# A chain of mixers: part order of an output chunk, low parts in halves, roots and gates' sums moved ahead

## The reference, cut to what matters

```python
y = gla_mixer(x, ...)              # layer 0; layer 1: dsa_mixer(x, ...)
x = layer_norm(ALPHA * x + y, ln_g[i], ln_b[i])
x = x + (p[i] @ ple_w[i]) * jax.nn.sigmoid(x @ ple_gate_w[i])
...
h = rms_norm(x, norm_g) @ w_in     # the block after the layers
```

## Time and profile before

| | |
|---|---|
| median of 3 runs (lowest, highest) | 1513.79 us (1510.99, 1514.42) |
| the profiled execution: time, span | 1513.75 us, 1512.0 us |
| TensorE matmul busy | 1454.0 us, 96% |
| DVE, ACT, POOL busy | 619.2, 524.0, 553.9 us |
| mean granted clock of TensorE | 0.985 |

### The profile page before, as it was taken

One profiled execution on the slowest core, in us unless ns is written; L12 is line 12 of the kernel. 1 busy time (PEld: TensorE's weight loads), 2 busy tenths in 40 slices (PEclk: granted clock), 3 DMA queues, 4 the chain that ended last, 5 costly groups with the idle time before them and its releaser, 6 DMA issues.

```text
span 1512.0 us, 25079 instructions
## 1 busy us (share of the span) xinstructions
PE 1454.0 (96%) x10817; PEld 1269.4 (84%) x10817; DVE 619.2 (41%) x1296; ACT 524.0 (35%) x866; POOL 553.9 (37%) x235
## 2 busy tenths in 40 slices
PE   7999999999999999999999999998999999988898
PEld 7898886799998897778788899978988987768897
DVE  6032351124016335379655511454123512477424
ACT  3354223433113232333444421233434322563311
POOL 6433421133333225964373234323343342062211
PEclk9999999999999999999999999999999999998999
DMA  5222220022522123222110042223432222002111
GB/s 172 85 84 84 84 84 29 29 84 85 202 91 84 52 97 111 84 80 88 56 57 29 29 181 85 79 76 112 142 88 90 79 84 84 1 15 74 70 58 56
DMA packets 114669, 122.90 MB, mean 81 GB/s; under 512 B 12666, under 2 KB 107750, under 8 KB 114303
## 3 DMA queue, kind: packets, MB, share of 16 engines
q1 hardware_dynamic: 111008, 115.36, 23.5%
q10 hardware_dynamic: 3550, 5.94, 1.1%
HBM read 114.99 MB, written 6.31 MB: 80 GB/s over the span
## 4 chain that ended last, share of the span: by engine, by line
PE 90%; DVE 5%; ACT 2%; POOL 1%; issue 1%; ACTq 0%; DVEq 0%
PE ps L218 86%; PE ps L1454 1%; DVE x L1199 1%; DVE x L1194 1%; PE ps L1036 1%; DVE heads L2042 1%; PE ps L1460 0%; DVE qkT L2130 0%; ACTq L339 0%; ACT xT_high L909 0%; PE ps L278 0%; PE ps L900 0%; PE ps L3061 0%; POOL w_low L199 0%; PE ps L2649 0%
## 5 line engine op out<-in xcount | busy, mean ns | idle before, releaser
L199 POOL TENSOR_TENSOR w_low<-w_ring,w_high 128x2048 fp32r<-128x2048 f32 (+4 forms) x95 | 415.2, 4372 | 735.9 <-ACT w_high L184 722.8
L218 PE MATMUL ps<-w_high,xT_high 128*128 128x256 f32 (+1 forms) x1056 | 304.8, 289 | 9.0 <-POOL w_low L460 4.1
L218 PE MATMUL ps<-w_low,xT_high 128*128 128x256 f32 (+1 forms) x1056 | 299.2, 283 | 0.0
L218 PE MATMUL ps<-w_high,xT_low 128*128 128x256 f32 (+1 forms) x1056 | 299.1, 283 | 0.0
L184 ACT ACTIVATE w_high<-w_ring 128x2048 fp32r<-128x2048 f32 (+1 forms) x91 | 171.5, 1885 | 314.1 <-PE ps L218 310.0
L218 PE MATMUL ps<-xT_high,w_high 128*128 128x512 f32 (+1 forms) x600 | 241.3, 402 | 2.2 <-POOL w_low L199 1.2
L218 PE MATMUL ps<-xT_high,w_low 128*128 128x512 f32 (+1 forms) x600 | 237.0, 395 | 0.0
L218 PE MATMUL ps<-xT_low,w_high 128*128 128x512 f32 (+1 forms) x600 | 236.3, 394 | 0.0
L218 PEld LDWEIGHTS ps<-w_high,xT_high 128*128 128x128 f32 x1056 | 202.6, 192 | 16.0 <-issue 6.3
L218 PEld LDWEIGHTS ps<-w_low,xT_high 128*128 128x128 f32 x1056 | 202.7, 192 | 1.7 <-issue 1.7
L218 PEld LDWEIGHTS ps<-w_high,xT_low 128*128 128x128 f32 x1056 | 202.5, 192 | 0.0
(11 more groups left out here) (503 smaller groups left out, 2166.9 us busy)
## 6 DMA issues: line engine op xcount, KB each, us to landing
w_ring<-in_gla_w_in_dram SPq DMA_DIRECT2D x24, 1024.0 KB, 5.2
w_ring<-in_dsa_w_in_dram SPq DMA_DIRECT2D x19, 1024.0 KB, 5.0
w_ring<-in_w_in_dram SPq DMA_DIRECT2D x18, 1024.0 KB, 5.0
w_ring<-in_gla_w_out_dram SPq DMA_DIRECT2D x8, 1024.0 KB, 5.0
w_ring<-in_ple_gate_w_dram SPq DMA_DIRECT2D x8, 1024.0 KB, 4.8
w_ring<-in_dsa_w_out_dram SPq DMA_DIRECT2D x8, 1024.0 KB, 4.8
x_scratch<-x SPq DMA_DIRECT2D x4, 1024.0 KB, 6.7
w_ring<-in_w_out_dram SPq DMA_DIRECT2D x4, 768.0 KB, 4.6
```

The costliest lines, as they stand in the source:

```text
L199: ins = self.nc.gpsimd.tensor_tensor(low[:, part], whole[:, part], high[:, part].bitcast(F32), ALU.subtract)
L218: return self.nc.tensor.matmul(out, lhs, rhs, start=first, stop=last, skip_group_check=not check)
```

## The change

Six edits in one:

1. In the first output chunk, part j waits for low part 9 + j of g (of 16) instead of all four parts for 12, and `last_turns` stands behind part 1 of c = 0 instead of in front of c = 1.
2. The gate's first chunk is made low in two halves; TensorE takes the first four row tiles after the first half. POOL makes the low parts of later chunks only after all four tiles are normalised. ACT makes this chunk's high part in front of the split of the first tile.
3. On ACT the roots of tiles 0 and 1 stand behind square (1, 1), in front of the last sigmoid; the order behind the last sigmoid is final(0), root(2), final(1), square(1, 3), root(3).
4. On DVE scale(0), scale(1) and final(0) stand in front of the last gate; behind it square_sum(2), scale(2), final(1), square_sum(3), scale(3), final(2), final(3). The wait for the gain moves one tile ahead.
5. Chunk zA is made low in halves.
6. At `cum_copies` DVE does `branch_step` in front of `norm_heads`.

```diff
@@ phase_post, TensorE
-                pe.wait_ge(gT_made, gT_count + KI - 4)
                 for n in range(LAST):
...
                         if n == 0 and c == 1:
-                            last_turns(pe)
                             pe.wait_ge(*gT_done)
                         w = g.chunk(pe, first + 2 * n + c)
                         for j in range(NT):
+                            if n == 0 and c == 0:
+                                pe.wait_ge(gT_made, gT_count + KI - 8 + j + 1)
                             part(w, n, c, j).then_inc(sem["y_part"], add("y_part", 1))
+                            if n == 0 and c == 0 and j == 1:
+                                last_turns(pe)
...
-                        w = g.chunk(pe, gates + HALVES * n + half)
+                        first_chunk = n == 0 and half == 0
+                        w = g.chunk(pe, gates + HALVES * n + half, (sem["half_low"], past["half_low"] + 1) if first_chunk else None)
...
                             for k in range(KD):
+                                if first_chunk and j == 0 and k == KD // 2:
+                                    w = g.chunk(pe, gates)
@@ phase_post, ACT
+                g.split_high(act, gates + 1)
                 high(0)
-                g.split_high(act, gates + 1)
                 high(1)
...
-                        if j == NT - 1:
+                        square(1, j - 1)
+                        if j == NT - 2:
                             root(0)
-                        square(1, j - 1)
+                            root(1)
...
                 if then_norm:
-                    root(1)
+                    final(0)
+                    root(NT - 2)
+                    final(1)
                     square(1, NT - 1)
-                    root(NT - 2)
-                    final(0)
                     root(NT - 1)
-                    final(1)
                     g.split_high(act, gates + HALVES * NH + RING)
@@ phase_post, DVE
+                    if then_norm and i == NH * NT - 1:
+                        scale(0)
+                        scale(1)
+                        final(0)
                     dve.wait_ge(sem["gate_sigmoid"], past["gate_sigmoid"] + i + 1)
...
-                        if i == NH * NT - 1:
+                        if i == NH * NT - 2:
                             dve.wait_ge(sem["next_gain_landed"], past["next_gain_landed"] + 16)
-                            scale(0)
...
                 if then_norm:
-                    scale(1)
-                    square_sum(NT - 1)
-                    final(0)
                     scale(2)
                     final(1)
+                    square_sum(NT - 1)
                     scale(3)
@@ phase_post, POOL
+                g.split_low(pool, gates + 1, halved=gates)
+                pool.wait_ge(sem["normed"], past["normed"] + NT)
                 g.split_low(pool)
@@ phase_project, TensorE (and the same switch to the whole chunk at k == KD // 2)
+                    opening = i == 0 or c != tiles[i - 1][0]
+                    halved = opening and c == w2["zA"]
...
+                        w = g.chunk(pe, c_in + c, (sem["half_low"], past["half_low"] + 1) if halved else None)
@@ phase_project, DVE
+                    if i == cum_copies:
+                        branch_step(i)
                     norm_heads(i - heads_from)
-                    branch_step(i)
+                    if i != cum_copies:
+                        branch_step(i)
@@ phase_project, POOL
-                g.split_low(pool)
+                g.split_low(pool, halved=c_in + w2["zA"])
```

More of the change, by code:

```diff
@@ L1869, in _ @@
                 for i, (c, col, width, j, engine, what) in enumerate(tiles):
-                    if i == 0 or c != tiles[i - 1][0]:
-                        w = g.chunk(pe, c_in + c)
+                    opening = i == 0 or c != tiles[i - 1][0]
+                    halved = opening and c == w2["zA"]
+                    if opening:
+                        w = g.chunk(pe, c_in + c, (sem["half_low"], past["half_low"] + 1) if halved else None)
                     if i == 0:
@@ L1885, in _ @@
                     for k in range(KD if width else 0):
+                        if halved and k == KD // 2:
+                            w = g.chunk(pe, c_in + c)
                         if j is None:
```

## The result

The changed kernel takes 1493.03 us (median of 4 runs, 1492.37 to 1494.13) against 1513.40 us before (now 4 runs, 1510.99 to 1514.42): ratio 0.9867, 95% interval 0.9855 to 0.988, 20.4 us. The forecast was 1496.2 us, 17.5 us less, with an own range of 1493 to 1499, so the result stands at its lower edge.

A forecast was written before the change was run, and what follows sets the result against it. TensorE, busy 96% of the span, was taken as the bound, leaving its pauses and clock. Savings of 5.7, 7.8, 2.2, 1.3 and 0.5, together 17.5 us, off 1513.75 gave 1496.2 us; own range 1493 to 1499, 8 in 10: 1492.5 to 1502.

The forecast's parts named there:

- A: First output chunk, first layer: two TensorE waits and a clock fall go; 5.7 us saved, bounds 1.7 and 6.
- B: Gate's first chunk, both layers: waits for low part and third tile go; 3.9 us a layer, 7.8 in all.
- C: End of second layer: new orders shorten TensorE's wait for x_scaled; 2.2 us saved, bounds -1 and 3.9.
- R3: Rival, second layer's end: a table switch costs more than its 1.28 us; 1498.1 to 1499.4 us; chance 0.10.
- D: Chunk zA in halves: TensorE's wait for its low part goes; 1.3 us saved, bounds 0 and 1.4.
- E: Gates' sums ahead of a head product: wait on a_tok moves two tiles on; 0.5 us saved, bounds 0 and 2.0.
- R2: Rival, first output chunk: the turns' chain stays late, A worth 1.9 instead of 5.7; 1500.0 us; chance 0.09.
- R4: Rival: TensorE's clock stays low after a new broken stretch, kernel slower, 1517 us and more; chance 0.03.
- R5: Rival, whole kernel: unseen waits meet the gains, under 3 us remain, about 1512 us; chance 0.05.
- R1: Rival, gate's first chunk: POOL collides with the second tile, B worth 1.9 a layer; 1500.2 us; chance 0.09.

The follow-up runs named there:

- e5: Also experiment 2: kernel before with only the part-by-part waits in the first output chunk, last turns still in front of the second chunk; 1511.53 us (one run).
- e7: The changed kernel run once more, nothing altered; 1493.76 us, ratio 0.9862.
- e9: Also experiment 6: changed kernel without halves and POOL's new wait for the gate's first chunk, ACT's early high part kept; 1493.46 us, ratio 0.9867.
- e2: Also experiment 3: kernel before with only ACT's high part of the gate's first chunk put ahead of the first tile's split; 1504.76 us, ratio 0.9943.
- e8: Changed kernel plus sixth early embedding inside tile 2's product and DVE's running-maximum steps in front of the head product; 1491.44 us, ratio 0.9847.
- e4: Kernel before with only the orders of roots, scales and splits at the second layer's end changed; 1509.25 us, ratio 0.9974.
- e3: Also experiment 4: kernel before with only the gate's first chunk's low part in halves and POOL's wait for the fourth tile; 1506.96 us, ratio 0.9956.
- e1: Kernel before with only the first output chunk's edit (part-by-part waits, last turns behind part 1); 1506.79 us, ratio 0.9954.
- e6: Kernel before with only the gates' sums put in front of the head product on DVE; 1514.58 us (one run).
- e10: Kernel before with only POOL's wait for the fourth tile, low part whole; 1509.27 us (one run).

## Why the prediction was right, point by point

- **A, 5.7 forecast, 5.94 measured (5.96 alone).** The waits and the cover came as worked out: low parts of the turns done at 383.7, wanted at about 387.2. What the sum took in full, the 1.5 us of clock, is a matter of chance (experiment 2): the trace of before had the fall, as five of seven with this pause, so this part of the hit is partly luck. Without the fall A would be worth about 4.4 us (5.94 less 1.5).
- **B, 3.9 a layer forecast, 4.30 and 3.97 measured.** Of the 4.30, 0.3 arise behind the turn of the fourth tile; e7 and e9 haven't got them and gain 4.0. The times in it hold within a few tenths: first half, held pass (1.87 us), free second pass. What was not seen is that the early high part alone does it (experiments 3 and 6). The text counted POOL's new wait as harmless, and it is; it is also useless.
- **C, 2.2 forecast, 3.5 measured (3.5 alone).** The mis-sized term. The second product's start was right to 0.01 us, and at full clock the working gave 2.9. Subtracted were 0.7 for a fall of the clock that came in e7, e8 and e9 and not in the changed kernel or in e4. Where it did come it cost nothing by the start of the third tile's product: that stands 61.98 us behind the turns of the fourth x tile in the changed kernel and in e9, 61.97 in e7, 61.99 in e4. In e7 the slower turns and first product only filled waits for DVE that the changed kernel has there. Before, it is 64.79 us, so the gain up to there is 2.8 us. The other 0.7 us arise between there and the turns of w_sgu, where nothing was changed: this stretch takes 59.2 us in five traces (the changed kernel, e2, e4, e5, e7) and 59.9 in the other seven, before, e8 and e9 among them. C itself is 2.8 us against this trace of before, 0.6 above the forecast.
- **What C also does, and the prediction did not see.** In the kernels with the old order the same distance is not fixed: 63.6 us in e3, 64.8 in before, e1 and e2, 65.2 in e6, 65.6 in e5 and e10. DVE's scaling of the last tile and POOL's next low part start within 0.3 us of each other there, first in before and then in e5:

```profile
1051.96 1.29 DVE L1227 SCALAR_TENSOR_TENSOR x_scaled<-x,sumsq_x,p_tok 128x1024 f32<-128x1024 f32 x1
...
1050.03 5.49 DVE L1228 SCALAR_TENSOR_TENSOR x_scaled<-x,sumsq_x,p_tok 128x1024 f32<-128x1024 f32 x1
...
1049.84 4.60 POOL L199 TENSOR_TENSOR w_low<-w_ring,w_high 128x2048 fp32r<-128x2048 f32 x1 [17.71 <-ACT w_high L184]
```

  In before DVE is first by 0.16 us (POOL starts at 1052.12). In e5, e6 and e10 POOL is first by 0.1 to 0.2 us, the scaling takes 5.5 us, and TensorE waits another 1.3 to 1.5 us for it. With edit C it starts 1.65 us ahead of POOL in all five kernels. So C is worth 3.2 to 3.6 us against such a trace, and 1.7 against e3's.
- **R3 and the skill's price of a table load.** Each of the added loads took 1.28 us and nothing behind it (1027.17 to 1028.46, where the sigmoid starts). The drain of 1380 ns that the Trainium skill adds for every switch ("ScalarE: Activation LUTs", What ACT_TABLE_LOAD costs) is not seen here: the measurement decides, R3 did not come, and C wasn't 0.3 us.
- **D, 1.3 forecast, 1.47 measured.** It wasn't tried alone, but the stretch from the turns of w_sgu to those of the gates takes 14.5 us in all four kernels with it (after, e7, e8, e9) and 16.0 in the eight without.
- **E, 0.5 forecast, 0.43 measured (0.41 alone).** The wait of 2.0 us moved to the turns of the maximum, 1.6 us in e6 and e9, as worked out. In the trace of the changed kernel it can't be seen, as a fall of the clock just ahead slowed TensorE by as much (1.6 us).
- **The total.** The five terms were forecast at 17.5 and are 19.6 us. Of the 2.1 us more, A's 0.2, B's 0.2, C's 0.6 and D's 0.2 are the change's (E is 0.1 less); 0.3 in B's layer 0 and 0.7 in C's stretch are not. A further 1.8 us of the spans' difference is none of it either, 0.74 in the first 30 us and 1.1 in the branches, in both of which the clock and the landing of inputs differ from run to run. R2, R4 and R5 did not come. R1 came near: DVE's second pass over tile two starts at 464.88 and POOL's first half at 465.70, so DVE was first by 0.8 us, and it was POOL's half that was longer, 2.72 us against the second's 2.39.

## What to carry to other kernels

When TensorE is bound and its pauses have different releasers, each pause is worth its length if the next thing on the path is worked out to arrive in time; work that out on every engine in list order, and a wait like that on the gates' sums shows that four fifths of it only move. Try the parts of an edit alone: one moved line of ACT made halves and an added wait superfluous. Where two engines exclude each other, look first whether the long instruction can start earlier: cut in two, it let the other engine in between here (experiment 4). And look for two instructions of such engines that start within a few tenths of a us: which comes first can change from one trace to the next.

## What the runs showed of the hardware

- DVE and POOL exclude each other on SBUF-SBUF work, for a tiny instruction too: a subtraction of 128 x 16 values took 3.25 us beside a POOL instruction, where it took 0.17 before with POOL idle. The Trainium skill ("SBUF — State Buffer", SBUF: two separate sides) says that the one which starts first holds the shared ports for its whole instruction. The traces agree: in e3 DVE's passes of 2.81 and 2.90 us end 1.1 us after a half of POOL's does, and where DVE was first, POOL's low part took 5.57 us (before, 1052.12) instead of 4.6.
- After the same pause of 2.23 us the clock fell to 1.2 GHz in five kernels and not in two, and around the gates' sums in five of twelve traces: behind the pause of 1.9 us on a_tok in e3, e4 and e10, and without any pause, 0.5 to 1.3 us behind the last of the tiny products, in the two traces of the changed kernel. Two traces of one program differ by 3.4 us at the low clock. Single traces that differ by 1 or 2 us in one stretch are no evidence of an edit.
- A table load of ACT starts as soon as the instruction ahead of it ends, not when its own activation is released: the load for the third root starts at 1030.66, the root at 1033.09.
